# Four 64x64 quadrants of TensorE in the triangular inverse of a DeltaNet scan

## The reference, cut to what matters

```python
a_strict = jnp.where(strict, jnp.einsum('bhnid,bhnjd->bhnij', k, k) * decay * beta[..., :, None], 0.0)
rhs = jnp.concatenate([k * (beta * jnp.exp(gc))[..., None], v * beta[..., None]], axis=-1)
sol = lax.linalg.triangular_solve(a_strict, rhs, left_side=True, lower=True, unit_diagonal=True)
```

## Time and profile before

| what | us |
|---|---|
| median of 3 runs (lowest, highest) | 4437.81 (4431.61, 4441.96) |
| the profiled execution | 4428.83 |
| its span, first to last instruction | 4427.1 |
| PE busy in the span | 4105.7 (93%) |
| PE weight loads busy | 3664.2 (83%) |
| DVE busy | 2336.3 (53%) |
| ACT busy | 1500.9 (34%) |
| POOL busy | 611.2 (14%) |
| mean granted TensorE clock, as a share of full speed | 0.962 |

### The profile page before, as it was taken

One profiled execution on the slowest core, in us unless ns is written; L12 is line 12 of the kernel. 1 busy time (PEld: TensorE's weight loads), 2 busy tenths in 40 slices (PEclk: granted clock), 3 DMA queues, 4 the chain that ended last, 5 costly groups with the idle time before them and its releaser, 6 DMA issues. The chain is left out here.

```text
span 4427.1 us, 107496 instructions
## 1 busy us (share of the span) xinstructions
PE 4105.7 (93%) x46477; PEld 3664.2 (83%) x46477; DVE 2336.3 (53%) x4078; ACT 1500.9 (34%) x2670; POOL 611.2 (14%) x755
## 2 busy tenths in 40 slices
PE   6999989999869998899998999989999779988998
PEld 5899977897749996899998999967988479977886
DVE  4555556454474434665556555564554554345434
ACT  4323343333342222433234333343332522223222
POOL 1221200330001000121211212100330010100000
PEclk8999999999979999999999999999999789999999
DMA  5433331000100003223223334321002000012332
GB/s 200 129 112 101 101 98 53 21 2 28 52 1 4 4 4 100 81 88 96 86 69 113 101 108 124 106 63 43 3 3 79 0 3 4 4 64 77 105 97 74
DMA packets 409087, 288.03 MB, mean 65 GB/s; under 512 B 13438, under 2 KB 366180, under 8 KB 408164
## 3 DMA queue, kind: packets, MB, share of 16 engines
q1 hardware_dynamic: 408676, 281.86, 20.9%
HBM read 270.27 MB, written 11.53 MB: 64 GB/s over the span
## 5 line engine op out<-in xcount | busy, mean ns | idle before, releaser
L793 ACT ACTIVATE w_hi<-w_raw 128x512 fp32r<-128x512 f32 (+1 forms) x724 | 406.0, 613 | 646.7 <-POOL w_raw L777 348.7
L800 DVE TENSOR_TENSOR w_lo<-w_raw,w_hi 128x512 fp32r<-128x512 f32 (+1 forms) x724 | 482.8, 708 | 173.4 <-ACT w_hi L793 173.4
L908 PE MATMUL PS<-x_hi,w_hi 128*128 128x384 f32 x1680 | 562.4, 335 | 1.2 <-DVE hid_flat L1089 1.2
L908 PE MATMUL PS<-x_lo,w_hi 128*128 128x384 f32 x1680 | 561.3, 334 | 0.0
L908 PE MATMUL PS<-x_hi,w_lo 128*128 128x384 f32 x1680 | 561.2, 334 | 0.0
L1174 DVE SCALAR_TENSOR_TENSOR arena<-PS,mod,arena 128x256 f32<-128x256 f32 (+1 forms) x336 | 198.4, 632 | 339.9 <-PE PS L921 339.8
L1089 DVE TENSOR_TENSOR hid_flat<-hid_flat,PS 128x384 f32<-128x384 f32 (+1 forms) x454 | 246.3, 557 | 245.5 <-PE PS L908 152.9
L921 PE MATMUL PS<-hidden_hi,w_hi 128*128 128x256 f32 (+1 forms) x1232 | 341.8, 347 | 7.7 <-DVE hidden_lo L1141 5.7
L921 PE MATMUL PS<-hidden_hi,w_lo 128*128 128x256 f32 (+1 forms) x1232 | 336.8, 343 | 0.0
L921 PE MATMUL PS<-hidden_lo,w_hi 128*128 128x256 f32 (+1 forms) x1232 | 336.8, 343 | 0.0
L908 PEld LDWEIGHTS PS<-x_hi,w_hi 128*128 128x128 f32 x1680 | 315.4, 188 | 1.9 <-DVE hid_flat L1089 1.9
(11 more groups left out here) (357 smaller groups left out, 8533.9 us busy)
## 6 DMA issues: line engine op xcount, KB each, us to landing
w_raw<-in_ffn_w_dram SPq DMA_DIRECT2D x512, 256.0 KB, 4.0
arena<-in_ada_w_dram SPq DMA_DIRECT2D x120, 512.0 KB, 5.7
arena<-in_w_in_dram SPq DMA_DIRECT2D x64, 512.0 KB, 3.9
arena<-in_ada_w_dram SPq DMA_DIRECT2D x6, 2048.0 KB, 14.7
arena<-in_w_out_dram SPq DMA_DIRECT2D x16, 512.0 KB, 4.4
h_save<-arena SPq DMA_DIRECT2D x16, 384.0 KB, 2.9
arena<-h_save SPq DMA_DIRECT2D x2, 3072.0 KB, 15.0
w_raw<-in_ffn_w_dram SPq DMA_DIRECT2D x32, 128.0 KB, 2.3
```

Source lines behind the costliest of these rows:

```text
L793: nc.scalar.activation(w_hi[:, high_place(n, what, j), 0:size], w_raw[:, load_of[what] % 2, place, 0:size], ACT.Copy).then_inc(w_high_read ...
L800: nc.vector.tensor_tensor(w_lo[:, b, place, 0:size], w_raw[:, b, place, 0:size], w_hi[:, high_place(n, what, j), 0:size].bitcast(F32), ALU ...
L908: mm = pe.matmul(PS[:, 4 * b + bank, 0:half], w[wo], x_split[xo][:, j, k, 0:half], start=(k == 0 and q == 0), stop=(k == KH - 1 and q == 2))
```

## The change

Heads 2 and 3 are moved to the other two quadrants of the array. Their matmuls read from one half and write the other half of the partitions (`ACROSS`, `lands`). The second product takes them back, so X stays where it was. The four quadrants are used in turn: head 0 low and high, head 2 low and high, then heads 1 and 3 (`FOUR_TILES`). Heads 0 and 1 write one PSUM bank and heads 2 and 3 the next (`two_banks`, 256 columns a head). So the first product now has banks 4g and 4g+1, and the turn of X and the second product share banks 4g+2 and 4g+3.

The PE stream of a level becomes: turn of X(l-1) then first product of level l for g = 0, the same two for g = 1, then the second product for g = 0, 1. The last turn keeps the old two quadrants and one bank (4g+2). Since banks 4g+2 and 4g+3 must be free before the first turn, it waits for `attn_ready` and `kst_ready`; L1925 is moved on DVE from behind level 1 to directly behind L1909 of the same direction. The wait for `at_moved` goes from the first turn to the first product of level 1.

The core of the diff:

```diff
+        ACROSS = {0: HALVES[1], 64: HALVES[0]}
+        FOUR_TILES = [(u, p) for pair in ((0, 2), (1, 3)) for u in pair for p in HALVES]
+        def lands(u, p):
+            return p if u < 2 else ACROSS[p.start]
+        def two_banks(b, w):
+            return PS[:, b:b + 2, :].rearrange("p a c -> p (a c)").rearrange("p (u c) -> p u c", u=DN_H)[:, :, 0:w]
+        def level_blocks(b, l):
+            return two_banks(b, 32).rearrange("p u (b j) -> p u b j", j=1 << l)
...
             def times(b, width, lhs, rhs):
-                for u in range(DN_H):
-                    for p in HALVES:
-                        mm = pe.matmul(PS[p, b, u * width:(u + 1) * width], lhs(u, p), rhs(u, p), start=True, stop=True)
+                for u, p in FOUR_TILES:
+                    mm = pe.matmul(two_banks(b, width)[lands(u, p), u], lhs(u, p), rhs(u, p), start=True, stop=True)
                 return mm
...
+                    def turn_x(g, l):
+                        pe.wait_ge(x_ready[g], xs + l + 1)
+                        if l == 0:
+                            pe.wait_ge(attn_ready[g], it + 1)
+                            pe.wait_ge(kst_ready[g], own + 1)
+                        if l < n - 1:
+                            mm = times(4 * g + 2, 64, lambda u, p: XP[g][p, u, :], lambda u, p: id_c[p])
+                        else:
+                            for u in range(DN_H):
+                                for p in HALVES:
+                                    mm = pe.matmul(blocks(4 * g + 2, p)[:, u], XP[g][p, u, :], id_c[p], start=True, stop=True)
+                        mm.then_inc(x_turned[g], 1)
+                    def lower_times_x(g, l):
+                        pe.wait_ge(x_ready[g], xs + l)
+                        if l == 1:
+                            pe.wait_ge(at_moved[g], it + 1)
+                        for u, p in FOUR_TILES:
+                            mm = pe.matmul(level_blocks(4 * g, l)[lands(u, p), u], AT[g][p, u, p],
+                                           even(XP[g][p, u, :], l, "p"), start=True, stop=True)
+                        mm.then_inc(tx_summed[g], 1)
+                    def x_times_lower(g, l):
+                        pe.wait_ge(tx_masked[g], ts + l)
+                        pe.wait_ge(y_ready[g], yt + l)
+                        times(4 * g + 2, 32, lambda u, q: YP[g][q, u, :], lambda u, q: TP[g][q, u, :]).then_inc(xd_summed[g], 1)
+                    for l in range(1, n):
                         for g in range(2):
+                            turn_x(g, l - 1)
+                            lower_times_x(g, l)
+                        for g in range(2):
+                            x_times_lower(g, l)
+                    for g in range(2):
+                        turn_x(g, n - 1)
...
-                                ins = sc.activation(YP[g], blocks(4 * g), ACT.Copy)
+                                ins = sc.activation(YP[g], two_banks(4 * g + 2, 64), ACT.Copy)
...
                         v.tensor_tensor(ATTN[g], DMT[g], bank(4 * g + 2), ALU.mult).then_inc(attn_ready[g], 1)
+                        u = slice(g * DN_H, (g + 1) * DN_H)
+                        row = lambda t: bc(t[:, bass.ds(first + i, 1), u].rearrange("p o u -> p (o u)"), 2, [P, DN_H, P])
+                        dve.wait_ge(ks_ready[g], it + 1)
+                        v.tensor_tensor(AV[g], bank(4 * g + 3), row(begc), ALU.mult).then_inc(kst_ready[g], 1)
```

More of the change, by code:

```diff
@@ L1596, in even @@
             return v[:, :, :, 0, :] if axes == "p u" else v[:, :, 0, :]
-        def packed(t, l):
-            return t.rearrange("p (u b j) -> p u b j", u=4, j=1 << l)
         def blocks(b, p=slice(0, P)):
@@ L1771, in pe_dn @@
                     xs, ts, yt = XS * layer + n * (first + i), TS * layer + n * (first + i), y_count(layer, first + i)
[L1772 to L1788, removed]
-                        for g in range(2):
[L1790 to L1794, removed]
@@ L1856, in step @@
                             if l < n - 1:
-                                ins = sc.activation(YP[g], blocks(4 * g), ACT.Copy)
+                                ins = sc.activation(YP[g], two_banks(4 * g + 2, 64), ACT.Copy)
                             else:
                                 for p in HALVES:
-                                    ins = sc.activation(Y[g][p, :, p], blocks(4 * g, p), ACT.Copy)
+                                    ins = sc.activation(Y[g][p, :, p], blocks(4 * g + 2, p), ACT.Copy)
                             ins.then_inc(y_ready[g], 1)
@@ L1912, in step @@
                             dve.wait_ge(tx_summed[g], TS * layer + n * (first + i) + l)
-                            v.tensor_tensor(TP[g].rearrange("p u (b j) -> p u b j", j=1 << l), packed(PS[:, 4 * g + 1, 0:128], l),
+                            v.tensor_tensor(TP[g].rearrange("p u (b j) -> p u b j", j=1 << l), level_blocks(4 * g, l),
                                             level_mask(l), ALU.mult).then_inc(tx_masked[g], 1)
@@ L1918, in step @@
                             x = even(XP[g], l)
[L1919 to L1925, removed]
+                            v.tensor_tensor(x, x, level_blocks(4 * g + 2, l), ALU.subtract).then_inc(x_ready[g], 1)
                     for g in range(2):
```

## The result

The changed kernel takes 4453.84 us (median of 5 runs, 4451.63 to 4459.68) against 4437.81 before: ratio 1.0045, 95% interval [1.0034, 1.0056], slower by 16 us. The forecast was 4387 us, with a range of 4374 to 4422. So it is a miss, with the wrong sign.

A forecast was written before the change was run, and what follows sets the result against it. TensorE's pace with small matmuls was taken as the bound. Four levels save 4.55 us, less 0.21 at the entry and 0.12 at the exit: 4.22 a step, 50.7 over 12 steps, 4437.8 to 4387 us; range 4374 to 4422.

The forecast's parts named there:

- The pace of four quadrants: Small matmuls of the levels: all four quadrants run side by side, an estimated 14.6 ns a pair.
- C: Quadrants with common rows take turns, so a level's PE work stays at 2.8 us: +5 us, 4443 us; chance 0.09.
- D: In a row half, loads can't run beside the other quadrant's matmul, 0.11 us a pair: +150 us, 4588; chance 0.05.
- The chain of a level: Turn, first product, mask, second product and subtraction in sequence for one direction: 1.89 us a level against 3.03.
- ACT's copy: Copy of the turn in each level: ready at 0.95 us, before the mask's 1.07, so hidden by 0.12 us.
- Reading two banks: Two-bank reads of DVE and ACT in the levels: costed at nothing, possibly 0 to 0.1 us each.
- The entry: Start of a step's levels: first turn 0.78 us late behind the moved reads, level 2 reached 0.21 us later.
- The hop to each direction's first turn: At the entry, from DVE's end to PE's first turn: 0.11 us, as the turn now has three waits.
- PE's own work is 96 x 14.6 = 1.40 us: PE in one level: 1.40 us, DVE's 1.16, so a latency chain takes over as the bound.
- Rival B: Partial overlap: issue or supply of instructions holds a pair at about 20 ns, level about 2.2 us, 4403 us; chance 0.12.
- exit: End of a step's levels: 0.12 us lost, since direction 1 trails by 0.59 us and no longer by 0.47.
- Rival E: TensorE's clock falls from 1.00 in the levels for PE gaps of 0.1 to 0.4 us: about as C; chance 0.02.

The follow-up runs named there:

- after_entry: The changed kernel plus useless fp32 128x128 matmuls in the entry's two waits, four before the first turn, one before direction 1's: 4442.76 us, ratio 1.0018.
- reads_first: The kernel before, quadrants and banks untouched, with only the two K.S reads moved up and the first turn waiting for them: 4478.15 us, ratio 1.0101.
- smooth_four: smooth with the turns ahead of levels 3 to 5 again as sixteen 64x64 quadrant pairs a direction: 4431.73 us, ratio 1.0005.
- after_fill: The changed kernel plus four useless 512-column bf16 matmuls a level, ahead of direction 1's second product: 4439.38 us, ratio 1.0009.
- whole_fill: whole_turn plus four useless 512-column bf16 matmuls a level, ahead of direction 1's second product: 4482.98 us, ratio 1.0106.
- whole_entry: whole_turn plus useless fp32 128x128 matmuls in the entry's waits, four before the first turn, one before direction 1's: 4410.30 us, ratio 0.9938.
- smooth: Against the kernel before: entry and level 1 kept, four quadrants for products and whole 128x128 turns from level 2 on: 4397.84 us, ratio 0.9918.
- long_run: The kernel before plus 1280 matmuls that wait for nothing, over four, two and one quadrants, after layer 0's scan: 4522.43 us against 4433.78.
- whole_turn: The changed kernel with each turn as two 128x128 transposes instead of sixteen pairs, 142 PE instructions a level for 198: 4457.54 us, ratio 1.0056.
- two_quads: The changed kernel with heads 2 and 3 back in the two old quadrants; new order, banks and moved reads stay: 4442.74 us, ratio 1.0019.

## Why the prediction was wrong, point by point

**The pace of four quadrants: right.** 58 / 4 = 14.6 ns a pair was the estimate; 14.7 ns was measured. Rivals C and D are out: heads 0 and 2 read the same rows here, and their loads follow each other at that pace. What the text read from the earlier trace rows can be seen in the loads too, each of which is 0.135 us long (the 0.135 of its divisions):

```profile
887.63 0.13 PEld L1798 LDWEIGHTS PS<-arena 64*64 64x64 f32 x1
887.68 0.14 PEld L1724 LDWEIGHTS PS<-id_c,arena 64*64 64x64 f32 x1
887.68 0.13 PEld L1798 LDWEIGHTS PS<-arena 64*64 64x64 f32 x1
887.69 0.19 PEld L1724 LDWEIGHTS PS<-id_c,arena 64*64 64x64 f32 x2
887.74 0.14 PEld L1798 LDWEIGHTS PS<-arena 64*64 64x64 f32 x1
887.75 0.14 PEld L1724 LDWEIGHTS PS<-id_c,arena 64*64 64x64 f32 x1
887.80 0.48 PEld L1798 LDWEIGHTS PS<-arena 64*64 64x64 f32 x7
```

Those of L1798 (low to high) begin 50 to 60 ns apart while those of the turn run in low-low and high-high, and 58 ns apart behind them: (0.48 - 0.135) / 6.

**The chain of a level: right.** It said 1.89 us, with the second product 1.07 us behind the turn. The level without a break takes 1.93 (951.05 to 952.98), its second product is 1.08 behind the turn (952.13). ACT's copy stayed hidden. Reading two banks cost nothing: mask 0.291 us, subtraction 0.289 and copy 0.384 on average (after, L1939, L1945 and L1879; the copy of before 0.385).

**The entry: its length right, its effect missed.** From L1931 to level 2's turn it is 3.93 us (871.97 to 875.90), before 3.68 (871.08 to 874.76): 0.25 lost, 0.21 was forecast. The hop to each direction's first turn, taken at 0.11 us, is 0.12 (L1935 ends at 873.25 and 874.45, the loads begin at 873.37 and 874.57). The text followed PE's wait ahead of the first turn only as time on the chain. That it makes two waits, of 1.34 and 0.61 us, in which PE does nothing, and that the clock could answer to them, it did not price.

**"PE's own work is 96 x 14.6 = 1.40 us … so a latency chain takes over as the bound": here it failed.** The time of a level had a term for each quadrant's pace and one for the chain, and none for the supply of instructions. A burst of 96 pairs at 14.6 ns has to be supplied, and the supply gives a pair every 31.4 ns, so four levels in a row can't take 1.9 us each. Rival B named "the supply of them", but with a pair at about 20 ns, a figure that no row bore out, and a chance of 0.12. The earlier trace rows held the warning: 96 pairs in 3.02 us is 31.5 ns, and none of the rows shown was quicker for long. The check is in the five steps of after_entry at full clock: their breaks in the levels add up to 2.3 to 3.3 us, 2.8 on average, and without them each step is 33.5 to 33.6 us long, against 33.1 forecast. Supply thus cost 2.8 of the 4.22 us, 34 us over 12 steps; the remaining 0.5 us a step, 5 us over 12, is what chain, entry and exit came out longer together. Supply and this rest alone would have brought the kernel to about 4426 us: outside the range, but still faster than before.

**Rival E was priced too low, and for the wrong place; it made the sign.** It had 0.02, "about as C", for gaps of 0.1 to 0.4 us a level. The level at half clock really is no worse than C:

```profile
918.08:920.85 2.77, 2.77 (x96) 2.65 (x97) 0.96 (x4) 0.77 (x2) 2.77 (x5) 0.50 0.02 6
```

But the clock, once down, stays down for 3 to 20 us and takes the 128-wide products behind the levels along; these the text left out. The steps of after average 38.66 against the 36.34 of after_entry at full clock: 2.3 us a step, 28 us over 12. The sum is then -50.7 + 34 + 5 + 28 = +16 us. By its making it is 12 times the step's growth of 1.38 us, so it checks only that the loss lies in the steps, and the measured +16.0 fits it better than could be expected: the profiled executions differ by 22.8. Nor do the two losses stand side by side in the trace: in the steps that run at half clock through the levels (from 948.28 and 986.15 on) PE has no break there, since it then takes a pair only every 27 ns (blocks of 16 loads begin at 918.46, 918.89 and 919.31). The division holds for this order alone: first the supply at full clock, then what the clock adds.

**What the clock's loss divides into.** Each of two causes brings the clock down by itself: the entry's waits (reads_first) and the breaks (smooth_four). In after nine falls of eleven come at the entry. Yet with the entry filled and the breaks left (after_entry) only 12 us of the 28 come back (ratio 1.0018 for 1.0045), since the clock then falls in the levels in five steps of ten.

**What stays open.** Why the clock falls in one step and not in the next of the same kernel; why after_fill's filler helped and whole_fill's hurt; whether it was the place or the kind of the filler that made whole_entry succeed where whole_fill failed, since both differ (fp32 128x128 at the entry, bf16 64x64 in the levels). That the entry matters rests on reads_first and smooth, which hold no filler.

## What to carry to other kernels

When parallel units are to shorten many small matmuls, ask first how many instructions a us the engine gets (here 256 in 4.02 us, 64 a us): if the stretch of before already stands near that rate, only fewer instructions help (a transpose of 128x128 for eight of 64x64; smooth_four, without it in levels 3 to 5, takes 35.24 us a step for 34.46), not more overlap. And price a longer wait of TensorE twice, once on the chain and once through the clock of all that follows (here 0.50 for 3 to 20 us): keep the waits as short as they were, or fill them. Check both with one kernel that issues without waits and one that only moves the wait.

## What the runs showed of the hardware

- PE's instruction supply: 256 instructions in 4.02 us, a few times in 3.5 to 3.7, whatever the quadrants (long_run). The breaks between the loads are 0.21 us with two quadrants and 2.08 with four in the rows above.
- Four 64x64 quadrants in fp32, two in each row half, take a pair every 14.7 ns (after, blocks at 878.89 and 879.12); one takes one every 58 ns.
- Two waits of PE of 1.34 and 0.6 us with some 0.6 us of work between them went ahead of a fall of TensorE's clock from 1.00 to 0.50 in half of the steps or more (after, reads_first, whole_turn); after 1.35 and 0.15 us it held (two_quads), and after a single one of 0.55 us (before, smooth, the ten full steps). Breaks of the supply in the levels went ahead of a fall in three steps of ten (smooth_four), each time one of 0.9 us and one of 1.2 to 1.5 us, some 4 us apart.
- Five useless matmuls a step, in waits that the step has anyway, were worth some 50 us. Filler in bf16 in the levels' short gaps made whole_turn slower by 22 us (1.0106 for 1.0056).
- Between the 128x128 loads and the 64x64 ones behind them there is a break of 0.17 us (smooth, L1805 to L1822, 96 times). A level has two of them, 0.34 of the 0.39 us by which smooth's level (2.32 us) is longer than the 1.93 seen with quadrants alone; that the change of tile is the reason is an estimate.
